# Top-64 steps moved among the scores, and two gate slots turned into rounded parts, in a two-layer hybrid decoder trunk

## The reference, cut to what matters

```python
p = x @ w_in                                   # att, gate, r/k/v and low-rank columns
# sparse attention: score every key for every query, keep the best 64
rel = relu(einsum('bqhd,bsd->bqhs', qi, ki))   # 8 index heads of 64
score = einsum('bqhs,bqh->bqs', rel, wi)
score = where(key_pos <= t, score, -inf)
_, idx = lax.top_k(score, 64)
# softmax attention (8 heads of 128) over the selected keys -> y_a
# RWKV-7 recurrence over 16 heads of 64 -> y_b
g_a, g_b = split(sigmoid(p_gate + b_gate))
x = layer_norm(alpha * x + (g_a * y_a + g_b * y_b) @ w_out)
x = layer_norm(alpha * x + conv_glu_ffn(x))
```

## Time and profile before

| | us |
|---|---|
| median of 3 runs (lowest, highest) | 1141.61 (1141.31, 1144.69) |
| the profiled execution | 1142.29 |
| its span in the trace | 1139.8 |
| PE busy | 1112.4 (98%) |
| DVE busy | 815.5 (72%) |
| ACT busy | 567.9 (50%) |
| POOL busy | 54.8 (5%) |

### The profile page before, as it was taken

How to read it: one execution, slowest core, us unless ns; L and a number is a source line. 1 busy time by engine, 2 the same in 40 slices (tenths; PEclk the granted TensorE clock), 3 DMA queues, 4 the chain that set the end, 5 groups by cost and what they waited for, 6 DMA issues and landing times.

```text
span 1139.8 us, 29793 instructions
## 1 busy us (share of the span) xinstructions
PE 1112.4 (98%) x12544; PEld 1013.9 (89%) x12544; DVE 815.5 (72%) x1483; ACT 567.9 (50%) x984; POOL 54.8 (5%) x49
## 2 busy tenths in 40 slices
PE   7999999999999999999999999999999999999996
PEld 7978889888898899998898888888988988999985
DVE  2678777768576887784557886868785778777745
ACT  3653555545454465563246445555463545555531
POOL 0000000000000100000010000000000000000000
PEclk9999999999999999999999999999999999999998
DMA  7433131322375456556464322222223745555651
GB/s 278 163 111 117 62 104 64 98 76 86 123 248 185 155 196 187 187 186 204 155 224 133 127 86 89 74 92 82 80 76 136 254 148 203 188 190 190 205 190 56
DMA packets 45516, 165.44 MB, mean 145 GB/s; under 512 B 5168, under 2 KB 5424, under 8 KB 45136
## 3 DMA queue, kind: packets, MB, share of 16 engines
q1 hardware_dynamic: 42736, 154.03, 40.9%
q0 software_dynamic: 1504, 7.47, 2.1%
q10 hardware_dynamic: 1152, 2.10, 0.6%
HBM read 160.44 MB, written 3.15 MB: 144 GB/s over the span
## 4 chain that ended last, share of the span: by engine, by line
PE 85%; DVE 10%; ACT 2%; POOL 1%; issue 1%; DMA 1%; DVEq 0%; SPq 0%; ACTq 0%
PE ps L740 22%; PE ps L741 20%; PE ps L742 19%; PE ps L897 10%; PE ps L1055 3%; PE ps L715 2%; PE ps L1109 1%; POOL g L678 1%; DVE ring_r L1653 1%; PE ps L1125 1%; DMA ring<-stream_dram 1%; PE ps L857 1%; PE ps L838 1%; PE ps L778 1%; PE ps L909 1%
## 5 line engine op out<-in xcount | busy, mean ns | idle before, releaser
L740 PE MATMUL ps<-x_tok_r,mid_hi 128*128 128x256 f32 x576 | 175.7, 305 | 0.5 <-DVE ring_r L1653 0.5
L742 PE MATMUL ps<-x_tok_r,ring_r 128*128 128x256 f32 x576 | 162.2, 282 | 0.0
L741 PE MATMUL ps<-yb_hi,mid_hi 128*128 128x256 f32 x576 | 162.1, 281 | 0.0
L740 PEld LDWEIGHTS ps<-x_tok_r,mid_hi 128*128 128x128 f32 x576 | 108.6, 189 | 9.4 <-issue 1.4
L1653 DVE TENSOR_TENSOR ring_r<-ring,mid_hi 128x1024 fp32r<-128x1024 f32 x80 | 96.9, 1211 | 19.5 <-ACT mid_hi L1251 19.2
L1251 ACT CAST mid_hi<-ring 128x1024 fp32r<-128x1024 f32 x80 | 83.8, 1048 | 52.0 <-PE ps L742 41.9
L741 PEld LDWEIGHTS ps<-yb_hi,mid_hi 128*128 128x128 f32 x576 | 108.9, 189 | 0.7 <-issue 0.7
L742 PEld LDWEIGHTS ps<-x_tok_r,ring_r 128*128 128x128 f32 x576 | 108.9, 189 | 0.0
L1901 DVE TENSOR_TENSOR rs_ks_r<-ring,tha_kkn_r 128x1024 fp32r<-128x1024 f32 x44 | 53.9, 1224 | 20.8 <-ACT tha_kkn_r L1303 20.8
L1901 DVE TENSOR_TENSOR w_lo<-ring,w_hi 128x1024 fp32r<-128x1024 f32 x42 | 51.4, 1225 | 21.0 <-ACT w_hi L1303 20.9
L1901 DVE TENSOR_TENSOR X_Y_r<-ring,arc_r 128x1024 fp32r<-128x1024 f32 x42 | 51.3, 1221 | 20.6 <-ACT arc_r L1303 20.6
(11 more groups left out here) (477 smaller groups left out, 3382.8 us busy)
## 6 DMA issues: line engine op xcount, KB each, us to landing
ring<-stream_dram SPq DMA_DIRECT2D x281, 512.0 KB, 3.4
lora_w<-lora_dram POOLq DMA_DIRECT2D x2, 1536.0 KB, 7.0
W_bt<-rpar_dram POOLq DMA_DIRECT2D x4, 512.0 KB, 4.9
kt_V<-rpar_dram POOLq DMA_DIRECT2D x4, 512.0 KB, 7.4
x_tok<-x_dram SPq DMA_DIRECT2D x2, 512.0 KB, 4.1
v_saved_dram<-vs_dC ACTq DMA_DIRECT2D x4, 256.0 KB, 3.9
x_tok<-x_dram SPq DMA_DIRECT2D x1, 1024.0 KB, 5.0
vf<-v_saved_dram ACTq DMA_DIRECT2D x4, 256.0 KB, 3.3
```

Source lines behind the costliest of these rows:

```text
L740: pe.matmul(dst, lh, rh, start=start, stop=False)
L741: pe.matmul(dst, lh, rl, start=False, stop=False)
L742: return pe.matmul(dst, ll, rh, start=False, stop=stop)
```

## The change

Three edits, in both layers.

1. DVE's `topk` is cut into `top_of(t, first, end)` and `taken(t)`. The mask and steps 0 and 1 of the first token block go behind `scores_of(1)`; steps 2 and 3, and steps 4 and 5, go among the later scores and query rotations. Steps 6 and 7 and `taken(0)` stay where `topk(0)` stood.
2. Gate slots 4 and 5 (the third gate pair, which PE does last before round 0) become rounded parts, mids 8 and 9. PE's plain slots ahead of the rounds go from six to four.
3. ACT casts mids 8 and 9 behind gate 0. DVE makes their remainders behind step 2 of the second block's eight, and `prep_rn` moves from behind step 4 to behind step 5 (counted from 0).

```diff
-FIRST_MIDS = 2 + 3 * GB
+LAST_GATES = 2
+FIRST_MIDS = 2 + 3 * GB + LAST_GATES
...
-MIDS = [s for s in SLOTS if s[1] == "gate" and s[2] >= 2 * GATES_FIRST or s[1] == "rkv" and s[2] % KB >= GB
+MIDS = [s for s in SLOTS if s[1] == "gate" and s[2] >= 2 * GATES_FIRST - LAST_GATES or s[1] == "rkv" and s[2] % KB >= GB
...
 ACT
                 gate(l, 0)
+                mids_up_to(l, FIRST_MIDS)
...
 DVE
+                def top_of(t, first, end):
+
+                    kp = keep[:, t, 0:P * (t + 1)]
+                    if first == 0:
+                        dve.wait_ge(*dve_att(l, f"s{t}{H_IDX - 1}"))
+                        dve.tensor_tensor(keep[:, t, t * P:t * P + P], keep[:, t, t * P:t * P + P], C["causal"], ALU.add
+                                          ).then_inc(*dve_att.inc(l, f"causal{t}"))
+                    for i in range(first, end):
+                        dve.wait_ge(*dve_att(l, f"causal{t}" if i == 0 else f"rep{t}{i - 1}"))
+                        dve.max(small[:, 16:24], kp).then_inc(*dve_att.inc(l, f"max{t}{i}"))
+                        dve.wait_ge(*dve_att(l, f"max{t}{i}"))
+                        dve.match_replace(kp, small[:, 16:24], kp, TAKEN).then_inc(*dve_att.inc(l, f"rep{t}{i}"))
...
 second layer (l = 1)
                     scores_of(0)
                     scores_of(1)
                     lora_w_low(2)
+                    top_of(0, 0, 2)
                     scores_of(2)
                     scores_of(3)
-                    mids_up_to(l, FIRST_MIDS)
+                    mids_up_to(l, FIRST_MIDS - LAST_GATES)
                     lora_low(2)
+                    top_of(0, 2, 4)
                     queries(0)
+                    top_of(0, 4, 6)
                     scores_of(4)
                     scores_of(5)
                     queries(1)
...
 first layer (l = 0)
                     scores_of(0)
                     scores_of(1)
+                    top_of(0, 0, 2)
                     queries(0)
+                    top_of(0, 2, 4)
                     scores_of(2)
                     scores_of(3)
-                    mids_up_to(l, FIRST_MIDS)
+                    mids_up_to(l, FIRST_MIDS - LAST_GATES)
+                    top_of(0, 4, 6)
                     queries(1)
                     scores_of(4)
                     scores_of(5)
                 rkv(l, 0, 2)
...
-                topk(0)
+                top_of(0, 6, 8)
+                taken(0)
                 prep_decay(r0)
                 prep_pend(r0)
                 prep_ss(r0)
-                topk(1, lambda: prep_rn(r0))
+                top_of(1, 0, 3)
+                mids_up_to(l, FIRST_MIDS)
+                top_of(1, 3, 6)
+                prep_rn(r0)
+                top_of(1, 6, 8)
+                taken(1)
                 prep_keys(r0)
                 prep_arc(r0)
                 prep_bk(r0)
```

More of the change, by code:

```diff
@@ L513, in trunk @@
         rope = lambda w: [f"{w}a", f"{w}"]
+        top = lambda t, i, j: sum([[f"max{t}{n}", f"rep{t}{n}"] for n in range(i, j)], [])
+        ends = lambda t: [f"sel{t}", f"selb{t}", f"keep{t}"]
         scores = lambda i: [f"s0{h}" for h in range(4 * i, 4 * i + 4)] if i < 2 else [f"s1{h}" for h in (2 * i - 4, 2 * i - 3)]
@@ L516, in trunk @@
                                          + scores(0) + scores(1)
-                                         + (scores(2) + scores(3) + rope("rq0") + scores(4) + scores(5) + rope("rq1") if l else
-                                            rope("rq0") + scores(2) + scores(3) + rope("rq1") + scores(4) + scores(5))
-                                         + sum([[f"causal{t}"] + sum([[f"max{t}{i}", f"rep{t}{i}"] for i in range(8)], [])
-                                                + [f"sel{t}", f"selb{t}", f"keep{t}"] for t in range(TT)], [])
+                                         + ["causal0"] + top(0, 0, 2)
+                                         + (scores(2) + scores(3) + top(0, 2, 4) + rope("rq0") + top(0, 4, 6) + scores(4)
+                                            + scores(5) + rope("rq1") if l else
+                                            rope("rq0") + top(0, 2, 4) + scores(2) + scores(3) + top(0, 4, 6) + rope("rq1")
+                                            + scores(4) + scores(5))
+                                         + top(0, 6, 8) + ends(0) + ["causal1"] + top(1, 0, 8) + ends(1)
                                          + sum([[f"lh{g}", f"lg{g}", f"mx{g}", f"rc{g}", f"pn{g}"] for g in range(GROUPS)], [])
@@ L2143, in scores_of, with taken @@
                         last.then_inc(*dve_att.inc(l, f"s{t}{h}"))
+                def top_of(t, first, end):
[9 more added lines that the diff above has]
+                        dve.match_replace(kp, small[:, 16:24], kp, TAKEN).then_inc(*dve_att.inc(l, f"rep{t}{i}"))
+                def taken(t):
+                    kp = keep[:, t, 0:P * (t + 1)]
+                    dve.wait_ge(*dve_att(l, f"rep{t}{TOPK // 8 - 1}"))
+                    dve.tensor_scalar(kp, kp, TAKEN / 2, -NEG, ALU.is_lt, ALU.mult).then_inc(*dve_att.inc(l, f"sel{t}"))
+                    dve.wait_ge(*dve_att(l, f"sel{t}"))
+                    dve.tensor_scalar(kp, kp, NEG, None, ALU.add).then_inc(*dve_att.inc(l, f"selb{t}"))
+                    dve.wait_ge(*dve_att(l, f"selb{t}"))
+                    dve.tensor_tensor(keep[:, t, t * P:t * P + P], keep[:, t, t * P:t * P + P], C["causal"], ALU.add
+                                      ).then_inc(*dve_att.inc(l, f"keep{t}"))
                 if l:
@@ L2176, in _ @@
                 rkv(l, 0, 2)
-                def topk(t, halfway=None):
-                    dve.wait_ge(*dve_att(l, f"s{t}{H_IDX - 1}"))
-                    kp = keep[:, t, 0:P * (t + 1)]
-                    dve.tensor_tensor(keep[:, t, t * P:t * P + P], keep[:, t, t * P:t * P + P], C["causal"], ALU.add
-                                      ).then_inc(*dve_att.inc(l, f"causal{t}"))
-                    for i in range(TOPK // 8):
-                        if i == 5 and halfway:
-                            halfway()
-                        dve.wait_ge(*dve_att(l, f"causal{t}" if i == 0 else f"rep{t}{i - 1}"))
-                        dve.max(small[:, 16:24], kp).then_inc(*dve_att.inc(l, f"max{t}{i}"))
-                        dve.wait_ge(*dve_att(l, f"max{t}{i}"))
-                        dve.match_replace(kp, small[:, 16:24], kp, TAKEN).then_inc(*dve_att.inc(l, f"rep{t}{i}"))
-                    dve.wait_ge(*dve_att(l, f"rep{t}{TOPK // 8 - 1}"))
-                    dve.tensor_scalar(kp, kp, TAKEN / 2, -NEG, ALU.is_lt, ALU.mult).then_inc(*dve_att.inc(l, f"sel{t}"))
-                    dve.wait_ge(*dve_att(l, f"sel{t}"))
-                    dve.tensor_scalar(kp, kp, NEG, None, ALU.add).then_inc(*dve_att.inc(l, f"selb{t}"))
-                    dve.wait_ge(*dve_att(l, f"selb{t}"))
-                    dve.tensor_tensor(keep[:, t, t * P:t * P + P], keep[:, t, t * P:t * P + P], C["causal"], ALU.add
-                                      ).then_inc(*dve_att.inc(l, f"keep{t}"))
                 def o_low(i):
```

## The result

The changed kernel takes **1148.12 us** (median of 9 runs, 1146.44 to 1151.33), the kernel before 1142.31 in the same series (9 runs, 1141.31 to 1145.07): ratio **1.0049**, 95% interval 1.0038 to 1.0061, so 4.3 to 7.0 us slower. The executions of one kernel lie up to 5 us apart, so medians are compared. The profiled execution took 1148.45, its span is 1146.4 (1139.8 before).

What follows compares the result with a forecast made beforehand. PE, busy 98% of the span, was taken as the bound, with DVE having nothing to spare at the stretch's end. Layer 0's +1.8 and layer 1's +2.4 gave +4.2 us, so median 1145.8, range 1142.9 to 1148.0.

Steps and rivals of the forecast that it cites:

- Scores, layer 0: Moved top-64 steps among layer 0's scores: partly hidden in DVE idle time, second v slot some 0.55 us later.
- The wait before the decay: DVE idles before the decay until ACT's `thw`: of 4.6 us freed, 0.97 is left in layer 0, none in layer 1.
- The next wait and the remainders: Layer 0: `prep_ss` waits for PE's sums of squares, leaving 0.5 us; two remainders add 2.28 us on DVE, casts in time.
- The norms' copy: DVE's `rnT` copy comes at 90.65 against 87.90 in layer 0; PE idles 2.0 us there, some 1.8 in layer 1.
- The end of layer 0: `kp` is 1.78 us later, grams start at 98.6, PE arrives at 98.0 and waits: layer 0 +1.8 us.
- Layer 1: PE idles 1.4 to 1.5 us at the turning of queries; `kp` and turning of v 2.5 later: +2.4 us.
- The clock: Rival: TensorE drops to half clock behind the new waits, 1.2 us each, 1147.0 with one, 1148.2 with both; chance 0.12.
- "Nothing has a fixed time, so the delay stays.": Behind the changed stretches, in the rounds, each engine's work hangs on the one before, so the full delay stays.

Runs made afterwards that it cites:

- after, shifted: Full change with 16 small matmuls put ahead of all the rest, against the full change: 1150.30 us, ratio 1.0064 to the kernel before.
- steps-only kernel: Edit 1 alone (top-64 steps moved, all six gate slots plain) against the kernel before: 1142.5 us, ratio 1.0002.
- parts only: Kernel before with gates 4 and 5 as rounded parts and their remainders, top-64 steps unmoved: 1150.46 us, ratio 1.0066.
- after: The changed kernel with all three edits, against the kernel before: 1148.12 us, ratio 1.0049.
- spread: Full change with second-block steps moved ahead of the decay and first-block steps placed by PE's slack: 1145.97 us, ratio 1.0021 to the kernel before.
- fill, steps only: Edit 1 alone, with second-block top-64 steps moved into the wait before the decay, against the kernel before: 1143.23 us, ratio 1.0000.
- steps only, shifted: Edit 1 alone plus 16 small matmuls in PE's early idle time, against the kernel before: 1146.95 us, ratio 1.0036.
- the fill with 8 or 24: Full change, second-block steps moved ahead of the decay, plus 8 or 24 small matmuls at the start: 1143.08 us or 1141.18 us.
- the fill with 16 or 24: Full change, second-block steps moved ahead of the decay, plus 16 or 24 small matmuls at the start: 1142.32 us or 1141.18 us.

## Why the prediction was right, and where it wasn't

Right in sign and in cause: the parts' remainders land on DVE, and a wait stands between what DVE gives up and what it gets. The size was +4.2 us; measured +5.8, which is above the +3.2 to +5.4 of its sum, and 1148.12 stands just above the 1148.0 at which its range ends (the kernel before came out 0.7 higher in this series).

- **Scores, layer 0.** The v slot's third pass 0.13 us later in a trace whose stretch begins 0.2 us earlier: a stall of 0.33 where 0.55 stood. The estimate for the release of a wait was too large.
- **The wait before the decay.** DVE idle 2.56 us (2.3 said) and 4.27 (4.3 said), both ended by ACT. Filling it turned the loss of the stretch into a gain, which is the test of this step.
- **The next wait and the remainders.** The second block's mask at 81.81 (82.25 said), remainders 2.35 (2.28), casts in time. Right.
- **The norms' copy.** At 90.05 (90.65 said); PE idle 1.56 and 1.40 us (2.0 and 1.8 said).
- **The end of layer 0.** This step failed in its reason. `kp` came 1.17 us later by the trace, 1.37 with the earlier start (1.78 said), and DVE alone would have given +1.4. But PE was the last, because its clock fell; the grams came 2.05 later. Two errors, one short and one long, made the +1.8 look right.
- **Layer 1.** Turning of the queries 3.07 later, of which 1.98 is the start of the layer (first row, against 622.27): a stall of 1.1 (1.4 to 1.5 said). `kp` +2.25 by the same count (2.4 to 2.5 said). Right within 0.2.
- **The clock.** The rival had a chance of 0.12 and a price of 1.2 us for each fall, and the clock fell in both layers. Its time for both, 1148.2, is nearly the one measured, by luck. It cost 1.07 in layer 0, as priced, and nothing in layer 1, where DVE's turn of v was later than PE even so. The slack that I gave the rival was `kp`'s, not that of v.
- **"Nothing has a fixed time, so the delay stays."** This is the step that failed for the total. Between the stretches the shift changed by -1.0 (the step of layer 0's last stage), and behind layer 1's last round by +2.8. The stretches together gave +4.7 (2.2 and 2.5; 2.1 and 2.5 in the trace of after, shifted). Of the rest of the +6.9 in the trace, +2.8 came with the packet of instructions, -1.0 with the stage's step, and +0.4 in small shifts. So the +4.2 was short of the stretches' 4.7, of which 1.07 is the clock, which the sum didn't have, and that the total came near is in part luck.

How much of the +5.8 is the change's own can only be estimated: by its stretches 4.7 us. Code shifts alone moved the steps-only kernel by 4.4 us and the full change by 2.2 (1148.12 and 1150.30), each between different series; by the ratios 3.9 and 1.7. What chooses the step of the last stage stays open, and so does what the packets cost elsewhere in amounts under 0.5 us.

## What to carry to other kernels

Before work is taken off a busy engine to make room for new work behind it, look for the next wait in that engine's order: what is freed ahead of a wait becomes idle time, unless something from behind the wait is moved into it. Read the saving and the cost by landmarks in the trace (starts of the same instruction, place by place), since the median also holds effects of places that the edit doesn't touch. Where differences of 0.3% matter, time each version with the code shifted by a few harmless instructions as well; otherwise the verdict may be on the shift. An idle time of PE that waits for nothing ("issue") is worth a look at the packets of kind "instruction" just ahead of it.

## What the runs showed of the hardware

- TensorE's clock fell to 1.2 GHz at waits of 1.40, 1.56, 2.67 and 3.03 us in dense work, each time for 3.4 us but once for 6.8 (parts only, layer 0). In after the passes were then 0.21 us apart and not 0.12. It didn't fall at others of 1.61 (spread, 100.5), 1.71 (fill, steps only, 268.1) and 2.28 us (steps only, shifted, 327.6). At the wait of 2.08 us at the layer norms it fell in 19 of 28 cases. In after PE had been at work again for 1.1 us when it fell in layer 0, and for 2.3 in layer 1. The Trainium skill (TensorE: Matmul & The Clock Gate, Part 1) says that an idle TensorE goes back to half rate; the rows agree, but by its length alone no wait between 1.4 and 2.3 us tells whether it will.
- The convolution stage steps by 5.65 or by 5.60 us a block for all its blocks (117.7 or 116.7 ns a pass), in the one trace of each kernel. Layer 0: 5.60 in after, after shifted, the steps alone, the parts alone and the fill with 8 or 24; 5.65 in the other eight. Layer 1: 5.65 in after shifted and the fill with 16 or 24; 5.60 in the other eleven. Over a stage that is 1.0 us. What chooses it is open.
- 16 tiny matmuls in idle time at the start of a kernel changed its time by 4.4 us out of 1142 (medians of 12 and 5 executions, which don't overlap).
- PE's instructions come in packets of 16 KiB, one for 256 instructions. PE never started a block sooner than 0.9 us behind the end of its packet, and in seven of 14 traces it stood 0.55 to 1.71 us for one.
- The same load landed about 1.2 us later in layer 1, and 2.2 in layer 0, when a packet of instructions stood 1.6 to 2.4 us behind the burst's first issue.
